# Hybrid decoder step on one core: retention and gated memory interleaved by tile, then softmax attention with all cache steps

## The reference

```
z = x @ w_in + b_in                       # 16 column groups
y_a = chunk_mlp(u_a, v_a)                 # A
y_b, r = retention(q, k, v, r0)           # B: scan over chunks of 128, state r
y_c, c, n, m = mlstm(q, k, v, i, f, ...)  # C: scan over chunks of 128, state c, n, m
y_d = fox_prompt(q, k, v, logf)           # D: causal softmax attention with forget gates
y_d = fox_sample(..., k_past, v_past)     # E: 64 sample tokens over 2048 cached positions each
x = LN(ALPHA*x + merged @ w_out);  x = LN(ALPHA*x + moe(x))
# retention, one chunk:
s = einsum(q, k) * decay;  o = einsum(s, v) + einsum(q, r) * q_dec
r = c_dec * r + einsum(k * k_dec, v)
# mlstm, one chunk: as retention, but with weights from a running maximum m_t of gates:
m_t = max(b + m, rowmax(b_t - b_s + i_s));  s = einsum(q, k) * exp(dmat - m_t)
h = num / max(|den|, exp(-m_t));  c = g_st * c + einsum(k * g_in, v)
```

## Time and profile before

| | |
|---|---|
| median of 3 runs | 1789.06 us (1775.97 to 1796.46) |
| the profiled execution's own time | 1780.62 us |
| its span, first to last instruction | 1778.8 us |
| mean granted TensorE clock | 0.889 of 2.4 GHz |
| PE busy | 1507.0 us, 85% |
| DVE, ACT, POOL busy | 636.7, 317.8, 130.0 us |
| input projection, layer 0 | 23 to 248 us |
| mixing stage, layer 0 | 248 to 510 us |
| output projection to router, layer 0 | 510 to 640 us |
| experts, layer 0 | 640 to 868 us |
| mixing stage, layer 1 | 1104 to 1367 us |

### The profile page before, as it was taken

How to read it: one execution, slowest core, us unless ns; L and a number is a source line. 1 busy time by engine, 2 the same in 40 slices (tenths; PEclk the granted TensorE clock), 3 DMA queues, 4 the chain that set the end, 5 groups by cost and what they waited for, 6 DMA issues and landing times.

```text
span 1778.8 us, 19022 instructions
## 1 busy us (share of the span) xinstructions
PE 1507.0 (85%) x7296; PEld 848.7 (48%) x7296; DVE 636.7 (36%) x1392; ACT 317.8 (18%) x663; POOL 130.0 (7%) x118
## 2 busy tenths in 40 slices
PE   4999998878969749999499999887887982999990
PEld 2455556555644424544244655654654451545440
DVE  1132134754653511111332404476466442111116
ACT  1001012322410101111111000333132010111112
POOL 0000100100000050000200010101000005000002
PEclk9999998777969869999699999988687995999995
DMA  8038543455531459998802302554462324899974
GB/s 290 0 119 237 146 125 121 139 160 111 138 146 43 142 201 341 370 375 319 306 0 72 123 6 93 130 171 131 108 132 87 105 112 172 328 370 365 369 267 171
DMA packets 135949, 317.58 MB, mean 179 GB/s; under 512 B 51396, under 2 KB 81604, under 8 KB 114756
## 3 DMA queue, kind: packets, MB, share of 16 engines
q1 hardware_dynamic: 106688, 187.44, 31.3%
q0 software_dynamic: 12672, 86.51, 15.9%
q10 hardware_dynamic: 16516, 42.63, 6.2%
HBM read 267.35 MB, written 49.19 MB: 178 GB/s over the span
## 4 chain that ended last, share of the span: by engine, by line
PE 61%; issue 16%; DVE 12%; DMA 6%; ACT 2%; POOL 2%; SPq 0%; POOLq 0%; DVEq 0%; ACTq 0%
PE ps L1716 20%; PE ps L2043 7%; PE ps L2001 6%; PE ps L2060 3%; DVE ring L1069 3%; PE ps L1820 3%; PE ps L1719 2%; DMA kbuf<-in_cache_k,idx_k 2%; PE ps L1783 2%; DMA ring<-in_w_out 1%; PE ps L1765 1%; DVE z L1069 1%; PE ps L1802 1%; PE ps L1749 1%; PE ps L1943 1%
## 5 line engine op out<-in xcount | busy, mean ns | idle before, releaser
L1716 PE MATMUL ps<-ring,xT 128*128 128x512 f32 (+1 forms) x896 | 369.5, 572 | 7.0 <-DMA ring<-in_w_in 6.2
L2043 PE MATMUL ps<-ring,z 128*128 128x512 f32 x608 | 270.9, 599 | 1.9 <-ACT z L810 1.9
L1716 PEld LDWEIGHTS ps<-ring,xT 128*128 128x128 f32 x896 | 170.7, 192 | 193.3 <-issue 181.3
L2043 PEld LDWEIGHTS ps<-ring,z 128*128 128x128 f32 x608 | 114.2, 193 | 132.2 <-issue 131.5
L810 ACT ACTIVATE ring<-ps 128x512 f32<-128x512 f32 (+2 forms) x186 | 96.1, 539 | 382.4 <-PE ps L1820 199.0
L1069 DVE TENSOR_TENSOR z<-ps,vbuf 128x512 f32<-128x512 f32 (+3 forms) x84 | 47.6, 570 | 306.3 <-PE ps L1716 274.0
L810 ACT ACTIVATE z<-ps 128x512 f32<-128x512 f32 (+2 forms) x154 | 80.0, 543 | 425.9 <-PE ps L2043 249.2
L2060 PE MATMUL ps<-ring,z 128*128 128x512 f32 x304 | 136.9, 593 | 2.3 <-DVE z L1573 2.3
L1069 DVE TENSOR_TENSOR z<-z,ps 128x256 f32<-128x256 f32 x38 | 16.0, 421 | 295.7 <-ACT z L810 295.7
L2001 PE MATMUL ps<-ring,xT 128*128 128x512 f32 x256 | 112.9, 601 | 3.0 <-DMA ring<-in_w_out 3.0
L1820 PE MATMUL ps<-tab,kbuf 128*128 128x128 f32 x512 | 95.6, 318 | 12.0 <-DMA kbuf<-in_cache_k,idx_k 6.8
(11 more groups left out here) (251 smaller groups left out, 1589.9 us busy)
## 6 DMA issues: line engine op xcount, KB each, us to landing
ring<-in_w SPq DMA_DIRECT2D x114, 1024.0 KB, 8.6
ring<-in_w_in SPq DMA_DIRECT2D x12, 2048.0 KB, 10.4
z<-expert_rows ACTq DMA_DIRECT2D x38, 512.0 KB, 9.0
expert_rows<-z ACTq DMA_DIRECT2D x38, 512.0 KB, 8.4
expert_rows<-zero SPq DMA_DIRECT2D x1, 12288.0 KB, 53.5
ring<-in_w_out SPq DMA_DIRECT2D x4, 2048.0 KB, 10.8
vbuf<-in_b_in SPq DMA_DIRECT2D x2, 1670.0 KB, 15.0
ring<-in_w_in SPq DMA_DIRECT2D x2, 1072.0 KB, 6.4
```

The lines of the kernel that those rows point to most:

```text
L1716: m = mm(ps[0:n, i % 4, 0:w], xTv[:, k, t * P:t * P + n], slab[at % 3][:, k, 0:w], start=(k == 0), stop=(k == KD - 1))
L2043: m = mm(ps[:, 2 + s, :].rearrange("p (w f) -> p w f", w=2), xgT[s][:, q, :], w13[s][:, :, q, :], start=(q == 0), stop=(q == KD - 1))
```

## The change

The mixing stage is put into two phases. **Phase 1** does retention and gated memory together, tile by tile: while one waits on an engine, the other's work can be issued. For this retention gets its own SBUF pieces (`cb_*` in ring slot 0) and its own banks (4, 6, 7 and half of 1), and gated memory takes 0, 1, 2, 3 and 5. No cache step is taken in phase 1. **Phase 2** does attention with all 73 cache steps: one in each of the four turnings and the four forget rows, then four in each of the 16 rounds, and one behind. The keys are turned into two banks in a fixed pattern (`K_BANK`: 0 and 2), the product follows its transposition by two steps, not one, `cache_values` and the softmax of a sequence move by one or two places, and keys are gathered in four quarters of 0.5 MB, each with a semaphore of its own. The prompt's state stores move behind ScalarE's part of the sample tile, with the sigmoid of `c_o` behind them, and the three gate signals become one.

```
+        QUARTERS = 4
-        CACHE_STEPS = 8 * (DEC_BATCH + 1)
-        B_STEPS, C_STEPS, D_STEPS = (1, 1, 1), (1, 1, 2, 1), (1, 1)
+        CACHE_STEPS = 8 * (DEC_BATCH + 1) + 1
+        K_BANK = (0, 2, 0, 0, 0, 2, 0, 2)
+        K_BANK_BEFORE = (2, 2, 2, 1, 1, 4, 2, 2)
...
# GpSimd
             for b in range(DEC_BATCH):
+                for q in range(QUARTERS if b < DEC_BATCH - 1 else 0):
+                    pool.wait_ge(e_kps, upto(e_kps, 8 * b + 2 * (q + 1)))
+                    gather_keys(b + 1, q)
                 if b > 0:
                     pool.wait_ge(e_pv, upto(e_pv, b))
                     gather(vbuf[:, :], cv, b, v_in)
...
# TensorE, one cache step
+                if 2 <= u < 8 * DEC_BATCH + 2:
+                    cache_scores(u - 2)
                 if i < DEC_BATCH:
+                    if g % 2 == 0:
+                        pe.wait_ge(k_in[g // 2], upto(k_in[g // 2], 16 * (i + 1)))
+                    if u >= K_BANK_BEFORE[g]:
+                        pe.wait_ge(e_ksb, upto(e_ksb, u + 1 - K_BANK_BEFORE[g]))
+                    if g == 5 and j >= 0:
+                        pe.wait_ge(e_pm, upto(e_pm, j + 1))
                     for a in range(4):
+                        m = tr(ps[:, K_BANK[g], a * P:(a + 1) * P], kv[:, ...], idn)
                     m.then_inc(e_kps, 1)
...
# TensorE, phase 1
+            c_rows(0); b_turn(0); b_scores(0)
+            for t in range(NP):
+                if t > 0:
+                    pe.wait_ge(c_cd, upto(c_cd, t))
+                turn_qk(t, "c_q", "c_k", 0, c_T)
+                pe.wait_ge(b_sw, upto(b_sw, t + 1))
+                inside(t, cb_sw, HD, b_value(t), 4)
+                from_state(cb_qkT, ret, HD, 6, b_out)
+                c_scores(t)
+                pe.wait_ge(c_mt, upto(c_mt, t + 1))
+                pe.wait_ge(b_kd, upto(b_kd, t + 1))
...             # retention's update into bank 1, b_up
+                c_lasts(t)
+                pe.wait_ge(c_sw, upto(c_sw, t + 1))
+                pe.wait_ge(c_vx, upto(c_vx, t + 1))
+                inside(t, sw, W, c_value(t), 0)
+                from_state(qkT, mem, W, 2, c_out)
+                pe.wait_ge(c_kd, upto(c_kd, t + 1))
...             # gated memory's update into bank 5, c_up
+                c_rows(t + 1)
+                pe.wait_ge(b_state, upto(b_state, t + 1))
+                b_turn(t + 1)
+                b_scores(t + 1)
...             # the sample tile: both groups, heads in turn
# VectorE, phase 1
+            for t in range(NP):
+                c_maxima(t); b_output(t); c_lasts(t); b_next_state(t); b_keys(t + 1)
...
+                c_weights(t); c_gates(t + 1); c_output(t); c_next_state(t); b_weights(t + 1)
+            c_maxima(NP); take_queries(cb_qm, 4, 1); c_lasts(NP); b_output(NP); c_weights(NP)
+            take_queries(qm, 0, 2); sample_keys(0, 0); c_output(NP); sample_keys(1, 0)
+            for h in range(1, HEADS):
+                sample_keys(0, h); sample_keys(1, h)
...
# TensorE, phase 2
             for t in range(NP):
                 turn_qk(t, "d_q", "d_k", 4 + 2 * (t % 2), d_T)
+                cache_steps(1)
             for h in range(HEADS):
                 mm(ps[:, 5 + 2 * (h % 2), :], ...)          # forget row
+                cache_steps(1)
             for m_ in range(NP * HEADS + 2):
+                more = m_ < NP * HEADS
+                if more:
                     logits(m_)
+                    cache_steps(1)
                 if m_ >= 2:
                     values(m_ - 2)
+                if more:
+                    cache_steps(1)
...             # the probabilities of round m_ - 1 are turned
+                if more:
+                    cache_steps(2)
```

More of the change, by code:

```diff
@@ L769, in gpsimd_layer @@
             pool.wait_ge(gate_sb, upto(gate_sb, 1))
-            for half in range(2):
-                gather_keys(0, half)
+            for q in range(QUARTERS):
+                gather_keys(0, q)
             pool.wait_ge(z_sb, upto(z_sb, NT * N_SLABS))
@@ L885, in cache_steps, with turned_b @@
                     cache_step(next(steps))
-            for t in tiles:
+            def turned_b(t):
                 n = rows[t]
@@ L891, in scalar_layer @@
                 src = ps[:, 4, 0:4 * n].rearrange("p (a n) -> p a n", a=4)
[L892 to L901, removed]
+                f(cb_qkT[:, 0:2, 0:n], src[:, 0:2], ACT.Copy).then_inc(b_Tsb, 1)
+                f(cb_qkT[:, 2:4, 0:n], src[:, 2:4], ACT.Copy, scale=SCALE).then_inc(b_Tsb, 1)
+            turned_b(0)
             for t in tiles:
@@ new lines, in vector_layer @@
+            V.memset(vx[:, :, HD:HD + 1], 1.0).then_inc(c_free, 1)
+            dve.wait_ge(c_free, upto(c_free, 1))
+            c_gates(0)
+            b_keys(0)
+            b_weights(0)
+            for t in range(NP):
+                c_maxima(t)
+                b_output(t)
+                c_lasts(t)
+                b_next_state(t)
+                b_keys(t + 1)
+                if t + 1 == NP:
+                    repeat_queries(cb_qd2, "b_q")
+                    repeat_queries(qd2, "c_q")
+                c_weights(t)
+                c_gates(t + 1)
+                c_output(t)
+                c_next_state(t)
+                b_weights(t + 1)
@@ new lines, in vector_layer @@
+            c_maxima(NP)
+            take_queries(cb_qm, 4, 1)
+            c_lasts(NP)
+            b_output(NP)
+            c_weights(NP)
+            take_queries(qm, 0, 2)
+            sample_keys(0, 0)
+            c_output(NP)
+            sample_keys(1, 0)
+            for h in range(1, HEADS):
+                sample_keys(0, h)
+                sample_keys(1, h)
+            link(tt(rs, rs, T("c_dec_s").unsqueeze(1).unsqueeze(3).to_broadcast([P, BP, HEADS, HD]), ALU.mult))
+            dve.wait_ge(km_used, upto(km_used, 2 * HEADS - 1))
@@ L1725, in tensor_layer, with scores @@
             pe.wait_ge(z_sb, upto(z_sb, NT * N_SLABS))
-            def scores(t, sem):
+            def scores(t, qk, bank, sem):
                 n = rows[t]
@@ L1759, in mixed, with from_state, from_sample_states @@
+            def from_state(qk, state, w, bank, sem):
+                for pair in range(PAIRS):
+                    for par in range(2):
+                        at = slice(par * HD, (par + 1) * HD)
+                        m = mm(ps[:, bank + par, pair * w:(pair + 1) * w], qk[at, pair, :], state[at, pair, :], start=True, stop=True)
                 m.then_inc(sem, 1)
-            def sample_update(w, val, place):
+            def from_sample_states(qm_, state, w, bank, sem):
+                pe.wait_ge(s_in, upto(s_in, 16 * 3 * DEC_BATCH))
@@ L1769, in tensor_layer, with c_scores, c_lasts @@
+            def c_scores(t):
+                pe.wait_ge(c_Tsb, upto(c_Tsb, 2 * t + 2))
+                scores(t, qkT, 2, c_sc)
+            def c_lasts(t):
+                n = rows[t]
+                mm(ps[0:n, 1, 0:2 * HEADS], T("last" if t < NP else "last_s", n), mtb[0:n, :], start=True, stop=True).then_inc(c_last, 1)
             pe.wait_ge(rope_done, upto(rope_done, 1))
@@ L1912, in tensor_layer @@
+            for bp in range(BP):
+                m = mm(ps[:, 3, CU + bp * HEADS:CU + (bp + 1) * HEADS], T("last_of", NS)[:, bp * P:(bp + 1) * P], ge[0:NS, HEADS:], start=True, stop=True)
+            m.then_inc(c_up, 1)
+            pe.wait_ge(b_state, upto(b_state, NT))
             pe.wait_ge(c_cd, upto(c_cd, NT))
```

460 lines of the change are left out of this document (214 added, 246 removed).

## The result

The changed kernel took 1805.28 us (median of 4 runs, 1800.27 to 1810.34) against 1785.03 us of the kernel before in the same comparison: a ratio of 1.0132 (95% interval 1.0086 to 1.0177), so **slower by 1.3%**. The profiled execution took 1810.34 us, with a span of 1808.5 us and a mean clock of 0.876; it is the slowest of the four.

What follows compares the result with a forecast made beforehand. TensorE, nearly always issuing but partly at half clock, was taken as the bound; phase 1 gains 66 us, phase 2 loses 64, the last sum gains more: 5.3 us a layer, 10.6 in all, so 1778 us by median, range 1730 to 1826.

Steps and rivals of the forecast that it cites:

- Bounds and the clock: Mixing stages: TensorE nearly always issues, but partly at 1.2 GHz, the level falling behind short gaps; gated memory is a chain.
- Phase 1: Retention and memory together: start 5 us, four tiles of 18, sample tile 35, 112 in all; 66 us gained a layer.
- Rival D: Phase 1: VectorE takes both lists in order, so the groups only add up, 21 us a tile: 1802 us; chance 0.05.
- Rival A: Phase 1: interleaving fills the gaps and keeps 2.4 GHz, tile 14.5 us, sample 27: 1734 us; chance 0.15.
- Phase 2's list: Phase 2: 63 us of cache work at full clock moved into attention's 84 us, which included 20 us of losses.
- (a): Phase 2's head: four turnings and first steps start at the half clock the sample tile leaves, +5 us.
- (b): Phase 2's start: 24 sample state stores in one burst delay keys, stall 5 us (0 to 14), plus 3 for level.
- Removed: Phase 2's end: the pure attention chain, where one step a round left TensorE idle, goes; 20 us taken off.
- (c): Phase 2, each sequence: TensorE waits at the maximum's spreading behind VectorE's softmax passes, about 1 us, 8 in all.
- The last sum at full clock: Last sum after phase 2: 5.34 us at half clock before, should run at full clock, 2.5 us less.
- B: Phase 2: narrow key steps stay at 1.2 GHz, 1824 us if half the moved work, 1870 if all; chance 0.15.
- C: Phase 2: feeding keys or VectorE's softmax sets the pace, each sequence 2 us longer, 1810 us; chance 0.10.

Runs made afterwards that it cites:

- e2: Changed kernel with three unused 128x512 products added on TensorE per phase 1 prompt tile, in the gap behind the last values' sum: 1780.57 us, ratio 1.0016.
- e1: Changed kernel with phase 1's interleaving undone, retention's four prompt tiles first, then gated memory: 1842.65 us, ratio 1.0323.
- e3: Changed kernel with two of each round's four cache steps ahead of the head norm's squares on VectorE: 1783.16 us, ratio 0.9993.
- e8: e3 with the memory group's 16 sample state stores held back until the 62nd piece of keys is turned: 1774.47 us, ratio 0.9954.
- e12: e3 without key and value gathers for sequences 2 to 8, only phase 2 to be read: phase 2 took 144.9 and 144.8 us.
- e9: Changed kernel with two unused 128x256 products on TensorE ahead of each spreading but the last, VectorE's order kept: 1795.47 us, ratio 1.0066.
- e7: e3 with keys gathered in two halves of 1 MB instead of four quarters of 0.5 MB: 1798.44 us, ratio 1.0053.
- e5: e3 with the memory weights ahead of retention's next state and keys on VectorE in phase 1: 1777.90 us, ratio 0.9960.

## Why the prediction was wrong

**The direction was wrong**: I had 0.29 on slower by over 1%. Point by point:

*Bounds and the clock.* Right. I wrote that the level falls behind short gaps, and then didn't apply it to the waits that I added, nor to the gaps that stayed.

*Phase 1: 18 us a tile, 35 for the sample, 112 in all.* Measured 17.08 us, three times alike, and 107 us, with the clock at 0.67. The gap between `c_lasts` and `c_sw` was there, 3.46 us against my 3, and e2 shows that the tile runs at full clock once it is filled. The gain was a little more than I forecast: attention begins 69 us earlier (426 to 357), not 66. Rival D is out by e1. Rival A did not come true, but e2 (14 us) shows that the tile of 14.5 us is real once the level holds.

*Phase 2's list: 127 us of work at full clock.* 129 to 130 by e3, e8 and e12. Right. (By the measure used there the old stage's 84 us lost 12 us to the level and not 9, so the same sum would give 124.)

*(a) and (b), head and stall: 5 and 8.* The stall was there, 14.83 us on the chain, and feeding with its level cost 7.5 us (e12). Right in size, and right in cause: the stores (e8). One reading behind it doesn't hold: rows 5 show 199 GB/s over 5.26 us, and neither an issue nor a landing, so they don't give the 5.3 us of a half.

*"Removed": the 20 us of idle and lower level that attention had before.* **This is the step that failed.** The sum takes all 20 off, since the attention chain at the end was to be gone, and puts nothing back for the last rounds. They still lose. The last 20 us before the last sum, in the kernel before, the changed kernel and e3:

```profile
490.40:510.40 20.00, 14.76 (x81) 9.77 (x81) 7.83 (x19) 5.59 (x10) 0.00 (x0) 0.57 0.00 1
505.65:525.65 20.00, 15.99 (x102) 10.15 (x101) 7.40 (x17) 5.33 (x9) 0.72 (x1) 0.65 0.30 106
488.61:508.61 20.00, 16.49 (x104) 11.07 (x103) 7.42 (x17) 5.34 (x9) 0.89 (x1) 0.66 0.30 106
```

That is 5.2 us of idle and 8.6 by the level before, 4.0 and 7.0 after, 3.5 and 6.8 in e3. Phase 2 by stretch, layer 0 / layer 1, each with idle + level (1 - clock, times the length):

| | first 40 us | between | last 20 us |
|---|---|---|---|
| forecast | 13 | 8 | 0 |
| changed kernel | 4.5 + 10.8 / 5.5 + 7.2 | 5.9 + 9.8 / 5.9 + 8.4 | 4.0 + 7.0 / 3.8 + 7.2 |
| e1 (same phase 2) | 4.2 + 3.6 / 5.6 + 6.8 | 5.8 + 1.9 / 5.8 + 2.0 | 3.5 + 6.8 / 3.5 + 6.8 |
| e2 (same phase 2) | 2.5 + 10.0 / 2.2 + 4.8 | 5.9 + 6.1 / 5.8 + 1.9 | 4.1 + 5.4 / 3.5 + 6.8 |
| e9 (waits filled) | 3.8 + 6.4 / 6.3 + 10.0 | 1.7 + 0.0 / 1.8 + 0.0 | 3.5 + 6.8 / 3.5 + 6.8 |
| e3 (maximum first) | 5.4 + 7.2 / 4.5 + 8.8 | 1.0 + 0.0 / 1.0 + 0.0 | 3.5 + 6.8 / 4.1 + 5.2 |

Over the six phases 2 with the changed kernel's code the last 20 us lose 10.4 us on average where the sum has nothing. It is not the feeding: without gathers (e12) it is 10.3. No experiment was aimed at this end, so what loses the level there stays open.

*(c), the waits at the spreading: 1 us each, 8 a layer.* **The smaller part of the miss.** The waits are 6.2 us, a little under their price. But I allowed for a lost level only behind the stall (3 us) and at the head (5), expecting "about the same losses in other places" and then pricing only some of those places. Behind these waits the level costs 5 us a layer: by e9's median, and by the middle column on average over the six, where it ranges from 1.9 to 9.8 with the waits the same; with the waits filled or gone it is 0.0 in all four phases shown. So the waits are what the level falls behind there, though not every time. I had named VectorE's order as their cause, with the round's softmax passes in front of the maximum; e3 leaves those in front and moves only the squares of the head norm, which I hadn't named, and the waits fall from 6.2 to 0.7 us. The engine was right, the passes were others.

*The sum put right.* Over the six phases 2: 148, and 10 for the last rounds, 3 for the middle (10.9 against 8), 1 for the list, less 2 at the head: 160, measured 160.7 on average. In the profiled execution, the slowest of four, it is 168.8 and 165.3. Measured there, the level cost 25.4 us in layer 0's phase 2 where the sum held 8, and idle was 14.4 where it held 13. What makes one execution lose more than another is not settled. That e3, with 152.4 us and 1783 in all, came near the forecast of 148 and 1778 is luck in part: without the waits that e3 takes away the forecast was 140, and the 10 us of the last rounds are most of the difference.

*The last sum at full clock, 2.5 us less.* It took 5.07 us in layer 0 and 6.64 in layer 1 of the profiled execution, and 3.67 in both layers of e1, e2 and e3: 1.7 us less than before where the level holds, and no gain over the two layers where it doesn't.

*Rivals.* B (phase 2 loses the level) is what happened, in a milder form: clock 0.83, above the 0.8 that I had set, with some 57 us at 1.2 GHz (2 x 0.17 x 168.8), and from another cause than I gave. Narrow work does not fall by itself: e3 and e9 held 1.00 for 94 us with the same steps. C's size, 1810 us, is right by luck: VectorE did make TensorE wait once a sequence, but that was in the forecast already, and it didn't set the pace; TensorE did, at the lower clock. That e7 made the halves cost 5 to 7.5 us a layer shows that feeding is not far from being a bound too.

*Where the expected gain went.* Phase 1 saves 69 us a layer and the moved work costs 68 in e3 (152 against 84). The change moves work from one place to another at about the same price; what is left is decided by waits and clock.

## What to carry to other kernels

When a change adds a wait to TensorE, price the wait and then the work behind it at the lower clock; here the second was nearly as much as the first, on average. When a sum takes a stage's old losses off, show for each place that its cause is gone: the last rounds kept theirs. Look at what the releasing engine does just before: two or three small passes that nobody was waiting for stood ahead of a maximum that everything waited for, and turning them round was worth 1.2%. And a shorter critical path can give nothing while the clock is low (e5), so test it again once the gap is closed or filled.

## What was not expected of the hardware

- Useless products made the kernel faster: with 24 of 128x512 in phase 1 it took 1781 us instead of 1805, 16 us of that in phase 1 itself, at a clock of 1.00 instead of 0.70 over two tiles.
- A gap shortened from 3.5 to 2.2 us left the granted clock lower, 0.50 instead of 0.70, though TensorE was busy for 28.1 of 34 us; with the fill, 25.5 busy of 34 us went at 1.00.
- The same code of phase 2 took from 154 to 169 us in six measured phases, with 11.5 to 15.2 us of idle and the rest of the difference by the level. What sets it off is open; so is how the kernel before would do with fills of its own.
